# A kernel of two hybrid layers: no drain on TensorE at the ends of weight panels

## What is computed

```python
h = rmsnorm(x, norm_pre)
pool_u, pool_gate, q, k, v, attn_gate = split(h @ w_in)
pool_out = pool_mixer(pool_u, pool_w, pool_scale) * silu(pool_gate)
attn_out = swa_sink_attention(q, k, v, attn_sinks) * silu(attn_gate)
x = x + rmsnorm(concatenate([pool_out, attn_out]) @ w_out, norm_post)

h = rmsnorm_2(x, attn_norm_g)
c_q, c_kv, k_rope, z_mla, q_dil, k_dil, v_dil, z_dil, g_mla, g_dil = split(h @ w_in_2)
y_mla = (mla_attention(...) * silu(z_mla)) @ w_o_mla
y_dil = (dilated_mixture(q_dil, k_dil, v_dil) * silu(z_dil)) @ w_o_dil
merged = sigmoid(g_mla + b) * y_mla + sigmoid(g_dil + b) * y_dil
out = rmsnorm_2(x + merged @ w_out_2, final_norm_g)
```

## Time and profile before

| | us |
|---|---|
| median of 3 runs | 1871.75 |
| lowest, highest | 1866.0, 1873.81 |
| the profiled execution | 1865.84 |
| its span, first to last instruction | 1864.0 |
| TensorE busy | 1772.9 |
| VectorE busy | 763.3 |
| ScalarE busy | 588.6 |
| GpSimd busy | 503.4 |
| mean granted clock of TensorE | 0.98 |

### The profile page before, as it was taken

The page is one execution under the profiler, slowest core; times in us unless marked ns, Lnnn a source line. Parts: engine busy times, 40 slices in busy tenths (PEclk is TensorE's granted clock), DMA queues, the critical chain, the costliest instruction groups (busy, mean ns, idle before and its releaser), DMA issues. The chain is left out here.

```text
span 1864.0 us, 22521 instructions
## 1 busy us (share of the span) xinstructions
PE 1772.9 (95%) x8928; PEld 1478.7 (79%) x8928; DVE 763.3 (41%) x1209; ACT 588.6 (32%) x1329; POOL 503.4 (27%) x396
## 2 busy tenths in 40 slices
PE   5999999999999999999999999999999999999998
PEld 4777777888777777889988899887777777788776
DVE  3240445444342215532155421442320777773723
ACT  4101455335330114421044201431111666661112
POOL 6114022044205220022200222020232633542320
PEclk9999999999999999989999999999999999999999
DMA  6113011332374110021100211024465554406332
GB/s 194 41 57 102 12 58 64 125 124 52 114 299 148 46 34 24 18 63 45 35 24 18 64 45 36 28 63 157 155 227 167 142 113 108 110 23 210 114 124 91
DMA packets 88520, 171.10 MB, mean 92 GB/s; under 512 B 19744, under 2 KB 27040, under 8 KB 88288
## 3 DMA queue, kind: packets, MB, share of 16 engines
q1 hardware_dynamic: 42992, 78.45, 15.0%
q10 hardware_dynamic: 45424, 91.22, 13.8%
HBM read 120.94 MB, written 48.69 MB: 91 GB/s over the span
## 5 line engine op out<-in xcount | busy, mean ns | idle before, releaser
L598 POOL TENSOR_SCALAR w_hi<-w_stage 128x1024 fp32r<-128x1024 f32 (+3 forms) x140 | 129.0, 929 | 1118.1 <-PEq L1052 530.1
L605 POOL TENSOR_TENSOR w_lo<-w_stage,w_hi 128x1024 fp32r<-128x1024 f32 (+3 forms) x140 | 267.2, 1916 | 8.9
L1047 PE MATMUL ps<-w_hi,h2T_hi 128*128 128x512 f32 x584 | 253.0, 433 | 2.2 <-issue 1.6
L1047 PE MATMUL ps<-w_lo,h2T_hi 128*128 128x512 f32 x584 | 239.6, 410 | 0.0
L1047 PE MATMUL ps<-w_hi,h2T_lo 128*128 128x512 f32 x584 | 239.5, 410 | 0.0
L1047 PEld LDWEIGHTS ps<-w_hi,h2T_hi 128*128 128x128 f32 x584 | 161.9, 277 | 16.3 <-issue 5.1
L1047 PEld LDWEIGHTS ps<-w_lo,h2T_hi 128*128 128x128 f32 x584 | 163.0, 279 | 9.7
L1047 PEld LDWEIGHTS ps<-w_hi,h2T_lo 128*128 128x128 f32 x584 | 161.6, 277 | 11.0
L2095 DVE TENSOR_TENSOR rope_cos_part<-ps,cos_dil 128x512 f32<-128x512 f32 x48 | 33.2, 692 | 321.0 <-PE ps L1047 296.9
L696 PE MATMUL ps<-h2T_hi,w_hi 128*128 128x512 f32 x384 | 154.8, 403 | 1.5 <-issue 1.4
L696 PE MATMUL ps<-h2T_lo,w_hi 128*128 128x512 f32 x384 | 154.4, 402 | 0.0
(11 more groups left out here) (273 smaller groups left out, 3438.1 us busy)
## 6 DMA issues: line engine op xcount, KB each, us to landing
w_stage<-in_w_in SPq DMA_DIRECT2D x76, 512.0 KB, 3.6
w_stage<-in_w_out SPq DMA_DIRECT2D x16, 512.0 KB, 3.8
gate_scr<-gate_tiles ACTq DMA_DIRECT2D x16, 512.0 KB, 3.2
gates<-gate_scr ACTq DMA_DIRECT2D x32, 256.0 KB, 3.2
dil_scr<-dil_out ACTq DMA_DIRECT2D x24, 264.0 KB, 2.1
dil_nums<-dil_scr ACTq DMA_DIRECT2D x24, 256.0 KB, 3.6
q_mla<-q_nope_scr SPq DMA_DIRECT2D x24, 256.0 KB, 4.5
k_mla<-k_nope_scr SPq DMA_DIRECT2D x24, 256.0 KB, 5.2
```

What stands on the lines that cost most here:

```text
L598: last = nc.gpsimd.tensor_scalar(hi_, raw_, 1.0, 0.0, ALU.mult, ALU.add)
L605: last = nc.gpsimd.tensor_tensor(lo_, raw_, hi_.bitcast(F32), ALU.subtract)
L1047: m = pe.matmul(ps[:, u % 2, :], toks(a, k), b[:, s, k, :], start=(k == 0 and b is wh and a is h2h), stop=(k == KT - 1 and a is h2l))
```

## The change

The 28 drains with `panel_used` are gone from TensorE. A table `last_use` names for every panel the semaphore that the last unit made from it counts up anyway, and the count. GpSimd waits for that one before it refills the place. For o0 there was no such count in the right order, so the last matmul of its last unit now counts up a new semaphore, `o0_done`. The drains of `phase_end` stay, the order on every engine stays, and no data move otherwise.

```diff
+    last_use = {index[name]: use for name, use in (
+        ("u", ("u_done", 8)), ("pgate", ("pg_done", 8)), ("kv", ("qkv_done", 4)), ("q", ("fill_done", 8)),
+        ("agate", ("fill_done", 12)), ("o0", ("o0_done", 1)), ("o1", ("y_done", TT)), ("c", ("c_done", TT)),
+        ("mla", ("prepared", len(PREP))), ("od", ("y2_done", 2 * KT)), ("om", ("y2_done", 4 * KT)))}
+    for i_, name in enumerate(GATES[0] + GATES[1]):
+        last_use[index[name]] = "g_done", 8 * i_ + 8
+    for u_, (g_, kind, _) in enumerate(D_UNITS):
+        last_use[index[f"{kind}{g_}"]] = "d_done", u_ + 1
@@ GpSimd, before panel p
             if p >= 2:
-                pool.wait_ge(*after("panel_used", p - 1))
+                pool.wait_ge(*after(*last_use[p - 2]))
@@ TensorE, first layer
-        pe.drain().then_inc(sem("panel_used"), 1)
         panel_ready("pgate")
...
-                if f in (7, 11):
-                    pe.drain().then_inc(sem("panel_used"), 1)
...
-            if half == 1 and part == 1:
-                m.then_inc(sem("y_done"), 1)
+            if part == 1 and (half == 1 or t == TT - 1):
+                m.then_inc(sem("y_done" if half else "o0_done"), 1)
@@ TensorE, gates
-            if u % 8 == 7:
-                pe.drain().then_inc(sem("panel_used"), 1)
@@ TensorE, dilated stage
             if part == 1:
                 m.then_inc(sem("d_done"), 1)
-                if u + 1 == len(D_UNITS) or D_UNITS[u + 1][:2] != (g, kind):
-                    pe.drain().then_inc(sem("panel_used"), 1)
```

More of the change, by code:

```diff
@@ L785, in qkv_unit @@
             wide_unit(name, ps[:, b, :], hTh, hTl, n, plain_cols(m)).then_inc(sem("qkv_done"), 1)
-            if u == 3:
-                pe.drain().then_inc(sem("panel_used"), 1)
         for u in range(5):
@@ L1016, in prep_unit @@
             m.then_inc(sem("prepared"), 1)
-            if x == len(PREP) - 1:
-                pe.drain().then_inc(sem("panel_used"), 1)
         for u in range(16):
@@ L1218, in y2_unit @@
             m.then_inc(sem("y2_done"), 1)
-            if r == 2 * KT - 1:
-                pe.drain().then_inc(sem("panel_used"), 1)
         fill = {n_t: (0,), n_t + 1: (1,), n_t + 2: (2,), n_t + 3: (3, 4)}
```

## The result

The changed kernel takes 1848.08 us (median of six runs, 1839.81 to 1852.32). Beside it the kernel before took 1871.85 us (six runs, 1866.0 to 1877.5). The ratio is 0.9872 with a 95% interval of 0.9843 to 0.9901: 23.8 us less. The forecast was 1862.6 us, and its range ended at 1855. The direction was right, the size was not.

A forecast was written before the change was run, and what follows sets the result against it. TensorE, busy 95% of the span, was taken as the bound. Terms of 5.7 (exposed drains), 0.7 (seven refills) and 2.7 (v panels) made 9.1 us off the 1871.75 median: 1862.6 us, range 1855 to 1869.

The forecast's parts named there:

- where a drain costs: At panel ends: queue time of about 4 us is free; the delayed matmul starts cost 0.50 us, 0.62 in the dilated stage.
- the twelve places that I counted as exposed: Behind kv, c, gm0, gm1, gd0, od, om, p0, u, zm, o0 and mla, removing drains saves 5.7 us together.
- Rival 3: At the exposed drains only the last matmul's tail of 0.16 us is won: 2.6 us, giving 1869.1; chance 0.10.
- the six at nothing: Drains behind pgate, o1, zd, gd1, p1 and first-block q save nothing; up to 0.5 us each, 3.0 in all, if exposed.
- the k panels: Behind k0, k1, k2 the rope_out wait grows some 0.4 us; transposes come only 0.1 us closer to the unit's end.
- GpSimd's start: At each refill GpSimd starts 0.10 us earlier against the unit's end, while TensorE's next work comes 0.42 to 0.62 earlier.
- the number of flips: Behind v0, v1, v2 VectorE may get ahead of GpSimd's third chunk; one flip of three likeliest, 2.7 us together.
- v1: a tie: 0.1 or 2.5: Behind v1 VectorE's L2102 and GpSimd's third L598 would both start at 925.07; gain 0.1 or 2.5 us.
- Rival 2: Behind the v panels two flips, or one plus some covered drains exposed: 11.5 us, giving 1860.3; chance 0.22.
- Rival 4: Longer TensorE waits before rotation transposes lower the clock: 1.7 us per dip, a loss from six more; chance 0.06.
- the refills that end the next wait themselves: Behind k0, k1, k2, q0, q1, q2 and agate only GpSimd's 0.10 us is gained each: 0.7 us together.

The follow-up runs named there:

- e5: The changed kernel with 30 drains added, one behind each gate unit from 18 to 47: 1854.72 us, ratio 0.9941 to the kernel before.
- e6: The changed kernel timed once more, beside the kernel before on the same chip: 1846.52 us, ratio 0.9899.
- e1: The changed kernel with all 28 drains back on TensorE, GpSimd still released by the last unit's own signal: 1864.56 us, ratio 0.9989 to the kernel before.
- e11: e12 with rope_sin_part written three more times in the rotation of the first units of q0 and q1: 1836.62 us, ratio 0.982 to the kernel before.
- e2: The changed kernel with only the nine drains of the dilated stage back: 1864.46 us, ratio 0.9987 to the kernel before.
- e3: The changed kernel with only the three drains behind v0, v1 and v2 back: 1862.36 us, ratio 0.9974 to the kernel before.
- e4: The changed kernel with GpSimd's refill chunks in the dilated stage waiting until the rotations they would disturb are over: 1829.23 us, ratio 0.9809 to the kernel before.
- e7: e12 with all 28 drains put back: 1842.37 us, ratio 0.9848 to the kernel before.
- e10: e12 without the hold on the refills behind v0, v1 and v2: 1827.88 us, ratio 0.9785 to the kernel before.
- e12: The same kernel as e4, timed again: 1827.55 us, ratio 0.9776 to the kernel before.
- e8: The changed kernel with only the refills behind k0, k1 and k2 waiting for the panel's last rotation: 1840.68 us, ratio 0.9863 to the kernel before.

## Why the prediction was off, by its own steps

**Right: where a drain costs.** The queue's 4 us are no cost, the step is, and 0.50 is what the panels' ends gave back. Matmul by matmul, the starts of the two profiles put the twelve places that I counted as exposed at 5.6 us, where I had 5.7. Rival 3, the tail alone, is out: in e5 a drain costs 0.33 to 0.46 at each of the thirty places.

**Wrong, but small: one of the six at nothing.** The drain behind q in the first block was exposed. I took the scores behind it to hang on the unit's end alone. But ScalarE copies the transposed probabilities first, and these come from TensorE's transposes right behind the drain; only then follows q1T. From q's last matmul to the scores it was 3.42 us (246.73 to 250.15) and is 2.95 (247.14 to 250.09), with a wait of 1.69 in both. So this drain gave its 0.46 us. In the changed kernel:

```profile
248.44 1.02 ACT L1333 ACTIVATE probsT<-ps 128x1024 f32<-128x1024 f32 x1 [0.68 <-PE ps L857]
...
249.36 0.59 ACT L1315 ACTIVATE q1T<-ps 128x512 f32<-128x512 f32 x1
...
250.09 1.13 PE L844 MATMUL ps<-k1T,q1T 64*128 64x256 f32 x8 [1.69 <-ACT q1T L1315]
```

The one behind o1 gave 0.10, and those behind pgate, zd, gd1 and p1 gave nothing, as predicted.

**Right: the k panels.** The transposes kept their distance from the unit's end (5.04 us against 5.03), and the wait took the drain's time. The new longer waits brought no low clock behind k0 in this profile: the stretch that had 0.83 in the earlier trace rows is at 1.00.

```profile
630.00:640.00 10.00, 7.68 (x35) 5.97 (x35) 4.87 (x4) 1.20 (x2) 9.21 (x6) 1.00 0.29 76
```

One profile settles little here: in that of e6, the same kernel, this stretch has 0.83 again.

**Nearly right: GpSimd's start.** I wrote that it would come 0.10 us earlier against the unit's end. It begins 0.06 us behind ScalarE's copy (684.11 against 684.05), before it was 0.10: 0.04 earlier. That lead decides nothing by itself (e1).

**Wrong: the number of flips.** The mechanism and its price held. Against ScalarE's copy of the last unit, the transposes came 2.46 us earlier behind v0, 2.30 behind v1 (917.93 to 929.04 before, 910.16 to 918.97 after) and 0.00 behind v2 (11.04 in both). I wrote 2.5, a tie, and 0.1. One step that failed is "v1: a tie: 0.1 or 2.5", which I took at 0.1: the sum had 2.7 where the trace has 4.8. The tie was decided by 0.08 us (917.29 against 917.37), and the same way in the second profile of the same kernel (e6, waits of 0.38 and 0.36). Rival 2 with its two flips, 1860.3, was nearer, and still 12 us too slow.

**Wrong: the clock, counted on one side only.** Rival 4 let longer waits cost clock, and no step asked what a wait that goes away gives back. The multiply that opens a unit's rotation marks the distance of two units. From q0's first unit to its second it went from 11.73 to 8.36 us: 3.37 less, of which 1.97 is the wait, and 1.40 goes with the clock of 0.84 turned to 1.00. From q1's first to its second it went from 10.38 to 8.71, all of it the wait. From the second to the third it went from 16.52 to 13.45, with no wait there, and the clock went from 0.66 to 1.00: 3.07. In all 4.5 us of clock at these two places in this pair of profiles. Over all runs the mean clock is 0.9842 instead of 0.9802, 0.0040 x 1600 = 6.4 us; in e6 5.8. e11 points to the cause from the other side: two waits put there on purpose, 3.4 us long, cost 6.5 to 9.1. The mean clocks go roughly with the waits for rope_out as well: 0.977 to 0.980 in the four kernels with 14 to 16 us of them (before, e1, e2, e3), 0.984 in the changed kernel with 13, 0.986 to 0.987 in the held kernels with 1.3 to 4.1 (e4, e7, e10, e12). But e8 has 3.9 us of waits and 0.9842, e5 12.6 and 0.9852. It is not one for one, then. In e7 and e10 the long step from the second to the third unit of q1 is there with no wait before it (16.48 and 16.52), and in e6 the one of q0 is, 16.50 instead of 15.06 behind a wait of 0.38. A wait makes a low stretch likelier, and which one comes with it is partly chance.

**The books.** The two profiles differ by 17.5 us. Place by place, the starts of the matmuls give 11.4 for drains and order: 5.58 for the twelve, 0.47 for the refills that end the next wait themselves (predicted 0.7), 0.56 for q and o1 (predicted nothing), and 4.76 behind the v panels (predicted 2.7). Their mean clocks, 0.9832 and 0.9799, make another 5.3 by the 1.6 for each 0.001, and 0.8 is not assigned. The 4.5 of clock behind v0 and v1 are not the whole exchange: the kernel before has low stretches behind k0 and k1 that the changed kernel has not, and the changed kernel has 0.66 from 250 to 260 and 0.87 from 50 to 60, where the kernel before has 1.00 both times. Over all runs at equal clock the change is 13 to 14 us, about 2 more than the 11.4. e1, with all drains back, has 2.4 of that kind, so the excess does not come from drains that I had sorted wrongly. What it is beyond the cheaper drain stays open; it is not much larger than the scatter.

So the steps that failed are two terms of the sum: the clock, which had no term at all and is worth 5 to 6 us, and v1's tie, taken at 0.1 where it gave 2.3. With the 0.56 of q and o1 and that excess of 2 they bring the 9.1 us of the sum to about 19, where the two profiles differ by 17.5 us and the medians by 23.8 and, in e6, 18.5.

**The lock.** The Trainium skill (SBUF — State Buffer, "SBUF: two separate sides") holds that a VectorE instruction with two SBUF inputs and a GpSimd instruction that reads SBUF exclude each other for the whole instruction, whoever starts first. The runs agree: 2.41 us beside GpSimd (631.93, the changed kernel) and 0.42 without it (628.87, e4), on the same instruction. The multiplies that read PSUM take 0.68 to 0.69 us beside GpSimd and without it.

## What to carry to other kernels

When an engine loses time before an instruction that shares a lock or a port, do not only price what is removed: write down which engine reaches the lock first afterwards, and by how much; half a microsecond on TensorE decided 2.5 us, twice. If GpSimd's work is not urgent, let it wait for the signal of the VectorE work that it would hold up, which here took the ratio from 0.9872 and 0.9899 to 0.9809 and 0.9776. And price a wait of TensorE with the clock that follows it, on both sides of the ledger.

## What the runs showed of the hardware

- The mean granted clock of one kernel moves between 0.975 and 0.989 from run to run, and its span goes with it (correlation -0.93), 1875.0 to 1847.5 us.
- Waits of 1.7 us, put into two places that had none, cost 6.5 to 9.1 us, about 4 of them the waits and what they delay and the rest a lower mean clock, 0.9846 against 0.9865 or 0.9872 (e11 against e4 and e12).
- 28 drains do not change the mean clock (0.9867 with them, 0.9872 without), though each leaves TensorE idle for 0.2 to 0.3 us.
- Between the units of two panels a drain with its count costs 0.50 us and one without 0.46; between two units of one panel it costs 0.33 to 0.42. An ordinary step is 0.23.
